# A hybrid attention trunk on one core: two more Strassen-like quads of weight tiles in each layer's down-projection, and their first weight sums made in HBM by DMA

## The chip, the cores and the metric

One NeuronCore of a Trainium2 chip runs the whole program. The metric is the device time of one execution in microseconds, the median of several. Engines are named as in the profile: PE (TensorE), DVE (VectorE), ACT (ScalarE), POOL (GpSimd), SP (SyncE, which here only issues DMAs).

## The reference

Two layers over x of 256 x 2048 in fp32. Each layer adds three sub-layers to x, each between RMSNorms: a mixer of 16 attention heads of three kinds behind one input projection, a cross-attention over 256 memory tokens, and a gated MLP. What the change touches is the last product of the MLP, of 256 x 4096 with a weight of 4096 x 2048:

```
def conv_ffn(h, w_up, conv_w, conv_b, w_down):
    ...
    gate, val = jnp.split(c, 2, axis=-1)
    return (jax.nn.gelu(gate, approximate=True) * val) @ w_down
```

## The kernel before

All weights are laid out on the host as one stream of **pieces** of 128 x 1024 fp32 (512 KB), 344 a layer, in the order of their use. SP loads piece p into the ring `raw` of 8 slots as soon as piece p-8 is free. For exact fp32 products every piece is split in two: ACT copies it into `w_hi` (a rounded form), DVE subtracts that from it into `w_lo`. Both have four slots (`SPL`), and PE multiplies hi x hi, hi x lo and lo x hi. A split waits on ACT until PE has used the split four before it (`split_free`), on DVE for ACT (`hi_ready`), and on PE for DVE (`lo_ready`). Each engine has its own queue in program order; semaphores are all that ties them together.

A layer has these stages: input projection with attention interleaved, output projection, memory keys, queries and values, its output projection, the up-projection (16 groups of 8 pieces) and the down-projection (64 pieces). In the up stage POOL makes one step of the convolution for each group (`up_c`, from DVE's `up_u`).

**The down stage.** It runs in two passes q of 1024 output columns, each of two groups of 512. Weight rows come in blocks j = 0 to 15 of 256, so a pass has 16 pairs of pieces (j, left) and (j, right). An ordinary pair costs PE 2 x 12 matmuls of 128 x 512. For the j in `SEVEN` the pair is instead handled as a **quad**: its two pieces are a 2 x 2 block matrix, and seven products instead of eight, as in Strassen's scheme, do the work, 21 matmuls in place of 24. This needs sums of the activations (made in the up stage, kept in HBM, loaded into `comb` by SP) and sums of the weights. A quad takes four splits, called A (the left piece), D (half of the right one), B (the first two weight sums) and C (two further sums). The weight sums are made by DVE in `psum_b` (an SBUF tile in spite of its name): `first_sums` adds two 128 x 512 pairs in one instruction, `other_sums` makes the other two one after the other. `PASS_HEAD`, `PASS_MID` and `PASS_TAIL` give the order of the blocks; from them come `DOWN_SPLITS` (88 splits of the stage) and `SEVEN_AT` (where the quads start). Between two quads there is always an ordinary pair. At the end of each pass DVE merges the product sums into the accumulators (`merge_sums`, `merge_odd`, `merge_even`), using `psum_b` too. Behind split 20 of the stage, ACT also issues the load of the last gain (`gain_f`, 1 MB) and loads a new activation table.

Of the kernel before, what the change touches and what calls it, by code (L numbers as in the profile page):

```python
# [414 lines left out]
def build(nc, stream, x_in, x_t_in, mem_in, mem_t_in, pos_in, consts_in, cols_in, rows_in, lam_in, gains_in, out):  # L415
    with ExitStack() as ctx:
# [74 lines left out]
        psum_b = sb("psum_b", [P, 4, 512], 88 * K)  # L491
# [170 lines left out]
        b_sums = sem("b_sums")  # L662
        m1_copied = sem("m1_copied")
# [94 lines left out]
        bias_hbm0 = nc.dram_tensor("bias_hbm0", (4 * H_A, 4, 8 * P), F32, kind="Internal").ap()  # L758
        comb_hbm = nc.dram_tensor("comb_hbm", (DEPTH * COMBS, P, 4 * 2 * P), F32, kind="Internal").ap()
# [8 lines left out]
        def _(sp):  # L768
# [24 lines left out]
            for l in range(DEPTH):  # L793
                for r in range(1 if l == 0 else l * rounds, l * rounds + narrow_rounds):
                    for j in range(4 if r == 1 else 0, RAW):
                        p = (r - l * rounds) * RAW + j
                        w = piece_width(p)
                        sp.wait_ge(lo_ready, raw_done(l, p - RAW))
                        sp.dma_start(raw[:, j, 0:w], stream[r * RAW + j][:, 0:w]).then_inc(landed[j], 16)
                with sp.Fori(l * rounds + narrow_rounds, l * rounds + P_DOWN // RAW + 1) as r:  # L800
                    for j in range(RAW):
                        sp.wait_ge(lo_ready, r * RAW + (l * (NSPLITS - NPIECES) + j + 1 - RAW))
                        sp.dma_start(raw[:, j, :], stream[r * RAW + j]).then_inc(landed[j], 16)

                def load_comb(n):

                    _, _, j, _, _ = DOWN_SPLITS[SEVEN_AT[n] - P_DOWN]
                    sp.wait_ge(*pieces_used(l, P_DOWN if n < 2 else SEVEN_AT[n - 2] + 4))
                    sp.wait_ge(comb_put, 16 * (l * COMBS + j // 2 + 2))
                    sp.dma_start(comb[:, n % 2].rearrange("p a b s -> p (a b s)").bitcast(F32),  # L810
                                 comb_hbm[l * COMBS + j // 2]).then_inc(comb_got[n % 2], 16)

                for p in range(P_DOWN + RAW, NPIECES):
                    sp.wait_ge(lo_ready, raw_done(l, p - RAW))
                    sp.dma_start(raw[:, p % RAW, :], stream[l * NPIECES + p]).then_inc(landed[p % RAW], 16)
                    for n, s in enumerate(SEVEN_AT):
                        if p == max(P_DOWN + RAW, P_DOWN + DOWN_SPLITS[s - P_DOWN][4] + 2):
                            load_comb(n)
# [530 lines left out]
        def _(act):  # L1349
# [48 lines left out]
            for l in range(DEPTH):  # L1398
# [4 lines left out]
                def split_down(s):  # L1403
# [8 lines left out]
                    elif kind == "D":  # L1412
                        act.wait_ge(*raw_landed(l, P_DOWN + i))
                        act.wait_ge(split_free, l * NSPLITS + s + 1)
                        act.activation(w_hi[:, s % SPL, 0:512], raw[:, i % RAW, 512:1024], ACT.Copy).then_inc(hi_ready, 1)
                    else:
                        n = l * len(SEVEN_AT) + seven(s - 2 if kind == "B" else s - 3)
                        act.wait_ge(b_sums, 3 * n + (1 if kind == "B" else 3))
                        act.wait_ge(split_free, l * NSPLITS + s + 1)
                        c = 0 if kind == "B" else 2  # L1420
                        act.activation(w_hi[:, s % SPL, :], psum_b[:, c:c + 2, :].rearrange("p a n -> p (a n)"),  # L1421
                                       ACT.Copy).then_inc(hi_ready, 1)
# [323 lines left out]

                for s in range(P_DOWN + SPL, NSPLITS + (2 if l < DEPTH - 1 else 0)):
# [24 lines left out]
        def _(dve):  # L1772
# [132 lines left out]
            for l in range(DEPTH):  # L1905
# [3 lines left out]
                def split_down(s):  # L1909
# [11 lines left out]
                    else:  # L1921
                        c = 0 if kind == "B" else 2
                        dve.wait_ge(hi_ready, l * NSPLITS + s + 1)
                        dve.tensor_tensor(w_lo[:, s % SPL, :], psum_b[:, c:c + 2, :].rearrange("p a n -> p (a n)"),
                                          w_hi[:, s % SPL, :].bitcast(F32), ALU.subtract).then_inc(lo_ready, 1)

                def first_sums(s):

                    ra, rb = [(P_DOWN + DOWN_SPLITS[s - P_DOWN + d][4]) for d in range(2)]
                    assert ra % RAW + 1 == rb % RAW  # L1930
                    n = seven(s)
                    if n == 0:
# [8 lines left out]
                def other_sums(s):

                    ra, rb = [(P_DOWN + DOWN_SPLITS[s - P_DOWN + d][4]) % RAW for d in range(2)]
                    n = 3 * (l * len(SEVEN_AT) + seven(s))
                    dve.wait_ge(b_sums, n + 1)
                    dve.tensor_tensor(psum_b[:, 2, :], psum_b[:, 0, :], raw[:, rb, 512:1024], ALU.add).then_inc(b_sums, 1)
                    dve.wait_ge(b_sums, n + 2)
                    dve.tensor_tensor(psum_b[:, 3, :], psum_b[:, 2, :], raw[:, ra, 512:1024], ALU.add).then_inc(b_sums, 1)
# [11 lines left out]
                def merge_odd(q):  # L1960
# [4 lines left out]
                    dve.tensor_tensor(acc(l, g, 0), acc(l, g, 0), psum_b[:, 0, :], ALU.add)  # L1965
                    st.done(dve.tensor_tensor(acc(l, g, 1), acc(l, g, 1), psum_b[:, 2, :], ALU.add))
                    dve.sem_inc(odd_merged, 1)

                def merge_even(q):
# [4 lines left out]
                    st.done(dve.tensor_tensor(acc(l, g, 1), acc(l, g, 1), psum_b[:, 1, :], ALU.subtract))  # L1974
# [432 lines left out]
                for s in range(P_DOWN + SPL, NSPLITS + (1 if l < DEPTH - 1 else 0)):  # L2407
# [28 lines left out]
        def _(pool):  # L2436
# [37 lines left out]
            for l in range(DEPTH):  # L2474
# [20 lines left out]

                pool.wait_ge(*item_done(l, ("O", HEADS - 1)))
# [14 lines left out]
                with pool.Fori(0, UPG // 2) as i:  # L2511
                    for half in range(2):
# [11 lines left out]
                        ins.then_inc(up_aff_ready, 1)  # L2524

# [128 lines left out]
```

## Time and profile before

| | |
|---|---|
| median of 3 runs | 1966.92 us (1966.91 to 1967.28) |
| profiled execution: its own time | 1967.23 us |
| span of the profile, first to last instruction | 1965.4 us |
| PE busy | 1952.6 us (99%) |
| DVE, ACT, POOL busy | 1506.6, 1138.2, 187.2 us |
| HBM traffic | 200 GB/s over the span |

The span lacks about 2 us around the first and last instruction. Busy time on PE is that of matmuls which overlap each other; the time from the start of one to the start of the next is what a run of them costs. The first layer's down stage runs from about 815 to 985 us, the second one's from about 1791 us to the end.

### The profile page before, as it was taken

What the parts mean: (1) busy time and instruction counts of PE and PEld (TensorE: products, weight loads), DVE (VectorE), ACT (ScalarE), POOL (GpSimd) and SP (SyncE); (2) the same over time, 40 slices, a digit from 0 to 9 for tenths busy, and PEclk for the clock granted to TensorE, in tenths of its full rate; (3) what the DMA queues carried; (4) which work ended last, traced back from release to release, by engine and by line L of the source; (5) the groups of instructions that cost most, each with busy time, mean ns of one, the idle gap of its engine ahead of it and who ended that gap; (6) DMA issues with size and microseconds to landing.
All of it is one profiled execution on the core that took longest, in us unless ns stands there. A gap on an engine that the chain in (4) does not pass through costs nothing.

```text
span 1965.4 us, 30737 instructions
## 1 busy us (share of the span) xinstructions
PE 1952.6 (99%) x10655; PEld 1680.0 (85%) x10655; DVE 1506.6 (77%) x2326; ACT 1138.2 (58%) x1770; POOL 187.2 (10%) x212
## 2 busy tenths in 40 slices
PE   9999999999999999999999999999999999999998
PEld 8888888888888888888888888888888888888886
DVE  7857777857777777788876577768587777778888
ACT  7655566657555555555566655556565555554654
POOL 0010000001222222200000000000012222222000
PEclk9999999999999999999999999999999999999999
DMA  8674558544656666576656444665446666565773
GB/s 319 200 204 155 170 211 241 198 152 169 202 192 207 198 206 200 203 274 240 220 150 229 153 155 160 213 218 196 155 153 205 203 201 209 188 205 210 267 251 135
DMA packets 111490, 393.94 MB, mean 200 GB/s; under 512 B 13140, under 2 KB 14560, under 8 KB 110048
## 3 DMA queue, kind: packets, MB, share of 16 engines
q1 hardware_dynamic: 105632, 368.36, 56.3%
q10 hardware_dynamic: 4448, 20.58, 2.7%
q0 software_dynamic: 1312, 3.70, 0.8%
q8 instruction: 61, 1.00, 0.2%
q14 instruction: 37, 0.30, 0.0%
HBM read 382.35 MB, written 10.24 MB: 200 GB/s over the span
## 4 chain that ended last, share of the span: by engine, by line
PE 98%; DVE 1%; issue 0%; ACT 0%; DMA 0%; DVEq 0%; SPq 0%; ACTq 0%
PE ps L971 24%; PE ps L974 12%; PE ps L881 12%; PE ps L883 11%; PE ps L882 11%; PE ps L893 11%; PE ps L896 5%; PE ps L1298 2%; PE ps L1297 2%; PE ps L1299 2%; PE ps L845 1%; PE ps L1248 1%; PE ps L1236 0%; PE ps L1234 0%; PE ps L1272 0%; PE ps L1260 0%
## 5 line engine op out<-in xcount | busy, mean ns | idle before, releaser
L1778 DVE TENSOR_TENSOR w_lo<-raw,w_hi 128x1024 fp32r<-128x1024 f32 (+2 forms) x660 | 778.6, 1187 | 323.0 <-ACT w_hi L1354 316.9
L1354 ACT ACTIVATE w_hi<-raw 128x1024 fp32r<-128x1024 f32 (+2 forms) x660 | 672.0, 1028 | 345.2 <-PE ps L974 219.7
L971 PE MATMUL ps<-h_t,w_hi 128*128 128x512 f32 x2032 | 639.0, 396 | 0.1
L974 PEld LDWEIGHTS ps<-h_t,w_lo 128*128 128x128 f32 x2032 | 382.1, 188 | 89.7
L974 PE MATMUL ps<-h_t,w_lo 128*128 128x256 f32 x2032 | 399.2, 278 | 0.0
L971 PEld LDWEIGHTS ps<-h_t,w_hi 128*128 128x128 f32 x2032 | 309.3, 189 | 0.3 <-DVE h_t L1796 0.3
L893 PE MATMUL ps<-h_t,w_hi 128*128 128x512 f32 x768 | 246.8, 403 | 0.0
L896 PEld LDWEIGHTS ps<-h_t,w_lo 128*128 128x128 f32 x768 | 144.3, 188 | 33.8
L2522 POOL TENSOR_SCALAR up_c<-up_u,cw 128x256 f32<-128x256 f32 x128 | 130.1, 1027 | 369.6 <-DVE up_u L2356 369.6
L896 PE MATMUL ps<-h_t,w_lo 128*128 128x256 f32 x768 | 151.2, 278 | 0.0
L883 PE MATMUL ps<-w_hi,act_t 128*128 128x512 f32 x320 | 124.5, 389 | 0.0
L881 PE MATMUL ps<-w_hi,act_t 128*128 128x512 f32 x320 | 124.5, 389 | 0.0
L882 PE MATMUL ps<-w_lo,act_t 128*128 128x512 f32 x320 | 124.5, 389 | 0.0
L893 PEld LDWEIGHTS ps<-h_t,w_hi 128*128 128x128 f32 x768 | 118.6, 189 | 1.7 <-DVE w_lo L1778 0.7
L881 PE MATMUL ps<-w_hi,h_t 128*128 128x512 f32 (+2 forms) x310 | 110.5, 356 | 0.1
L883 PE MATMUL ps<-w_hi,h_t 128*128 128x512 f32 (+2 forms) x310 | 108.2, 349 | 0.0
L882 PE MATMUL ps<-w_lo,h_t 128*128 128x512 f32 (+2 forms) x310 | 108.0, 348 | 0.0
L881 PE MATMUL ps<-w_hi,o_t 128*128 128x512 f32 x256 | 101.1, 395 | 0.0
L883 PE MATMUL ps<-w_hi,o_t 128*128 128x512 f32 x256 | 99.8, 390 | 0.0
L882 PE MATMUL ps<-w_lo,o_t 128*128 128x512 f32 x256 | 99.7, 390 | 0.0
L1421 ACT ACTIVATE w_hi<-psum_b 128x1024 fp32r<-128x1024 f32 x48 | 50.9, 1061 | 80.3 <-PE ps L883 80.0
L1699 ACT ACTIVATE s_sb<-s_sb,nmax 128x128 f32<-128x128 f32 x80 | 35.8, 449 | 76.2 <-DVE nmax L2295 75.4
(372 smaller groups left out, 2838.4 us busy)
## 6 DMA issues: line engine op xcount, KB each, us to landing
raw<-stream SPq DMA_DIRECT2D x640, 512.0 KB, 4.3
comb<-comb_hbm SPq DMA_DIRECT2D x24, 512.0 KB, 4.8
comb_hbm<-comb_out ACTq DMA_DIRECT2D x14, 512.0 KB, 6.1
raw<-stream SPq DMA_DIRECT2D x24, 288.0 KB, 3.4
raw<-stream SPq DMA_DIRECT2D x16, 262.0 KB, 6.0
gain_a<-gains_in ACTq DMA_DIRECT2D x4, 1024.0 KB, 6.5
m_x<-mem_t_in ACTq DMA_DIRECT2D x2, 2048.0 KB, 11.6
x<-x_in SPq DMA_DIRECT2D x4, 512.0 KB, 13.4
```

The lines of the kernel that those rows point to most:

```text
L881: pe.matmul(dst, s_hi, hi[:, j, :], start=f, stop=False, skip_group_check=True)
L882: pe.matmul(dst, s_hi, lo[:, j, :], start=False, stop=False, skip_group_check=True)
L883: mm = pe.matmul(dst, s_lo, hi[:, j, :], start=False, stop=e, skip_group_check=True)
L893: pe.matmul(acc(l, g, nt), hi[:, j, nt * P:(nt + 1) * P], src[:, c, :, :], start=f, stop=False, skip_group_check=True)
L896: mm = pe.matmul(acc(l, g, nt)[:, SEQ:2 * SEQ], lo[:, j, nt * P:(nt + 1) * P], src[:, c, 0, :], start=False, stop=e, skip_group_check=True)
L971: pe.matmul(ps[:, 4 * half + nt, :], hi[:, cc, nt * P:(nt + 1) * P], h_t[:, c, :, :], start=(c == 0), stop=False, skip_group_check=True)
L974: mm = pe.matmul(ps[:, 4 * half + nt, SEQ:2 * SEQ], lo[:, cc, nt * P:(nt + 1) * P], h_t[:, c, 0, :], start=False, stop=(c == KC - 1), skip ...
L1297: pe.matmul(dst, s_hi, hi, start=first, stop=False, skip_group_check=True)
L1354: act.activation(w_hi[:, slot, 0:width], raw[:, rslot, 0:width], ACT.Copy).then_inc(hi_ready, 1)
L1421: act.activation(w_hi[:, s % SPL, :], psum_b[:, c:c + 2, :].rearrange("p a n -> p (a n)"), ACT.Copy).then_inc(hi_ready, 1)
L1778: dve.tensor_tensor(w_lo[:, slot, 0:width], raw[:, rslot, 0:width], w_hi[:, slot, 0:width].bitcast(F32), ALU.subtract).then_inc(lo_ready, 1)
L2522: ins = pool.tensor_scalar(up_c[:, nt, :], up_u[:, nt, :], cw[:, 4 * nt + 2:4 * nt + 3], cw[:, 4 * nt + 3:4 * nt + 4], ALU.mult, ALU.add)
```

## The change

1. `SEVEN` gets a seventh block, j = 12: 14 quads a layer for 12. The order of the blocks changes, and in each pass there are now two places where two quads follow one another without an ordinary pair between. The stage has 92 splits.
2. The first weight sums are no longer made by DVE. POOL issues, for each quad, a copy of two half pieces from the stream into `b_hbm` and then, when that has landed, an accumulating DMA that adds the other halves. Eight quads are made at steps spread over the attention, output and memory stages (`SUMS_EARLY`), six in the up stage, one DMA a group; POOL's loop over the up groups is written out.
3. ACT issues a DMA (`load_sums`) that brings the sums of a quad, 512 KB, into `psum_b`, which is now two buffers, used in turn. `other_sums` stays on DVE and waits for that load; for a row of two quads both quads' other sums are made ahead of the first.
4. For the D piece of a quad only the half that is still used is loaded.

```diff
-SEVEN = [0, 2, 4, 6, 8, 10]
-PASS_HEAD, PASS_TAIL = [1, 3], [[14, 15], [12, 14, 15]]
-PASS_MID = [[5, 0, 7, 2, 9, 4, 11, 6, 13, 8, 12, 10], [0, 5, 2, 7, 4, 9, 6, 11, 8, 13, 10]]
+SEVEN = [0, 2, 4, 6, 8, 10, 12]
+PASS_HEAD, PASS_TAIL = [1, 3], [[14, 15], [13, 14, 15]]
+PASS_MID = [[5, 0, 7, 2, 4, 9, 6, 8, 11, 10, 13, 12], [0, 5, 2, 4, 7, 6, 8, 9, 10, 11, 12]]
+SUMS_EARLY = [(n, 48 + 11 * n) for n in range(4)] + [(4 + n, P_OUT + 6 + 11 * n) for n in range(3)] + [(7, P_MEMV)]
...
-        psum_b = sb("psum_b", [P, 4, 512], 88 * K)
+        psum_b = [sb(f"psum_b{i}", [P, 4, 512], at) for i, at in enumerate((88 * K, 104 * K))]
...
-                    sp.dma_start(raw[:, p % RAW, :], stream[l * NPIECES + p]).then_inc(landed[p % RAW], 16)
+                    c = 512 if P_DOWN + DOWN_FREED[p - P_DOWN] - 1 in SEVEN_AT else 0
+                    sp.dma_start(raw[:, p % RAW, c:], stream[l * NPIECES + p][:, c:]).then_inc(landed[p % RAW], 16)
...
+                def load_sums(n):
+
+                    m = l * len(SEVEN_AT) + n
+                    if n < 2:
+                        act.wait_ge(*pieces_used(l, P_DOWN - 4 * (1 - n)))
+                        act.wait_ge(b_made, 16 * (l + 1) * len(SEVEN_AT))
+                    else:
+                        act.wait_ge(lo_ready, l * NSPLITS + SEVEN_AT[n - 2] + 4)
+                    if DOWN_SPLITS[SEVEN_AT[n] - P_DOWN][1] == 1 and n % 2 == 0:
+                        act.wait_ge(odd_merged, 2 * l + 1)
+                        act.wait_ge(even_merged, 2 * l + 1)
+                    act.dma_start(psum_b[n % 2][:, 0:2, :], b_hbm[m]).then_inc(b_got[n % 2], 16)
+
+                load_sums(0)
                 for s in range(P_DOWN + SPL, NSPLITS + (2 if l < DEPTH - 1 else 0)):
                     up_tail(UPG // 2 - 1, 1, tail_at(s))
                     split_down(s)
+                    if s == P_DOWN + SPL:
+                        load_sums(1)
+                    for n in range(2, len(SEVEN_AT)):
+                        merged = DOWN_SPLITS[SEVEN_AT[n] - P_DOWN][1] == 1 and n % 2 == 0
+                        if s == max(SEVEN_AT[n - 2] + 5, down_end(1) + SPL + 1 if merged else 0):
+                            load_sums(n)
                     if s == P_DOWN + 20:
...
-                def first_sums(s):
+                def other_sums(s):
 
                     ra, rb = [(P_DOWN + DOWN_SPLITS[s - P_DOWN + d][4]) for d in range(2)]
-                    assert ra % RAW + 1 == rb % RAW
                     n = seven(s)
-                    if n == 0:
-                        dve.wait_ge(*pieces_used(l, P_DOWN - 4))
-                    else:
-                        dve.wait_ge(lo_ready, l * NSPLITS + SEVEN_AT[n - 1] + 4)
+                    m = 2 * (l * len(SEVEN_AT) + n)
+                    sums = psum_b[n % 2]
+                    if n > 1:
+                        dve.wait_ge(lo_ready, l * NSPLITS + SEVEN_AT[n - 2] + 4)
+                    dve.wait_ge(*first_sums(l, n))
+                    dve.wait_ge(*raw_landed(l, rb))
+                    dve.tensor_tensor(sums[:, 2, :], sums[:, 0, :], raw[:, rb % RAW, 512:1024], ALU.add).then_inc(b_sums, 1)
+                    dve.wait_ge(b_sums, m + 1)
                     dve.wait_ge(*raw_landed(l, ra))
...
-                    if s + 2 in SEVEN_AT:
-                        first_sums(s + 2)
-                    if s + 1 in SEVEN_AT:
+                    if s + 1 in SEVEN_AT and s - 3 not in SEVEN_AT:
                         other_sums(s + 1)
+                        if s + 5 in SEVEN_AT:
+                            other_sums(s + 5)
...
+                def sums_copy(n):
+
+                    m = l * len(SEVEN_AT) + n
+                    p = l * NPIECES + P_DOWN + DOWN_SPLITS[SEVEN_AT[n] - P_DOWN][4]
+                    pool.dma_start(b_hbm[m].rearrange("p a n -> a p n"), stream[p:p + 2, :, 0:512]).then_inc(b_put, 16)
+
+                def sums_add(n):
...
+                    pool.wait_ge(b_put, 16 * (m + 1))
+                    pool.dma_start(b_hbm[m].rearrange("p a n -> a p n"), stream[p + 1].rearrange("p (a n) -> a p n", n=512),
+                                   accum_op=ALU.add).then_inc(b_made, 16)
...
-                with pool.Fori(0, UPG // 2) as i:
+                for i in range(UPG // 2):
...
+                        n = len(SUMS_EARLY) + i
+                        if n < len(SEVEN_AT):
+                            (sums_add if half else sums_copy)(n)
```

**ACT, first layer's down stage, from the split of an ordinary pair to two quads later.** In the rows, an ACTIVATE from raw is the hi split of a piece (128x512: of a D piece), one from psum_b the B and C splits. Before, around the gain load:

```order
L1354 ACTIVATE w_hi<-raw 128x1024 x3
L1415 ACTIVATE w_hi<-raw 128x512
L1421 ACTIVATE w_hi<-psum_b 128x1024
L1753 DMA gain_f<-gains_in 128x2048
L1754 ACT_TABLE_LOAD
L1754 ACTIVATE lamv<-ident 128x1
L1421 ACTIVATE w_hi<-psum_b 128x1024
L1354 ACTIVATE w_hi<-raw 128x1024 x3
```

Of the change, the same place; psum_b_99 and psum_b_100 are the two buffers, and the three rows from the gain load on stand between the two splits 20 and 21 of an ordinary pair:

```order
L1365 ACTIVATE w_hi<-raw 128x1024
L1787 DMA gain_f<-gains_in 128x2048
L1788 ACT_TABLE_LOAD
L1788 ACTIVATE lamv<-ident 128x1
L1365 ACTIVATE w_hi<-raw 128x1024
L1772 DMA psum_b_99<-b_hbm 128x1024
L1365 ACTIVATE w_hi<-raw 128x1024
L1426 ACTIVATE w_hi<-raw 128x512
L1435 ACTIVATE w_hi<-psum_b_100 128x1024 x2
L1365 ACTIVATE w_hi<-raw 128x1024
L1426 ACTIVATE w_hi<-raw 128x512
L1772 DMA psum_b_100<-b_hbm 128x1024
```

The load of the second quad's sums (L1772, into psum_b_99) now stands behind split 21, four rows after the gain load.

**DVE, the same place.** A TENSOR_TENSOR into w_lo is a split's subtraction, one into psum_b makes weight sums. Before:

```order
L1778 TENSOR_TENSOR w_lo<-raw,w_hi 128x1024
L1938 TENSOR_TENSOR psum_b<-raw 128x1024
L1778 TENSOR_TENSOR w_lo<-raw,w_hi 128x1024
L1946 TENSOR_TENSOR psum_b<-psum_b,raw 128x512
L1948 TENSOR_TENSOR psum_b<-psum_b,raw 128x512
L1778 TENSOR_TENSOR w_lo<-raw,w_hi 128x1024
L1919 TENSOR_TENSOR w_lo<-raw,w_hi 128x512
L1924 TENSOR_TENSOR w_lo<-psum_b,w_hi 128x1024 x2
```

Of the change, splits 20 and 21, the sums of two quads, and the four splits of the first of them:

```order
L1812 TENSOR_TENSOR w_lo<-raw,w_hi 128x1024 x2
L1972 TENSOR_TENSOR psum_b_100<-psum_b_100,raw 128x512
L1975 TENSOR_TENSOR psum_b_100<-psum_b_100,raw 128x512
L1972 TENSOR_TENSOR psum_b_99<-psum_b_99,raw 128x512
L1975 TENSOR_TENSOR psum_b_99<-psum_b_99,raw 128x512
L1812 TENSOR_TENSOR w_lo<-raw,w_hi 128x1024
L1953 TENSOR_TENSOR w_lo<-raw,w_hi 128x512
L1959 TENSOR_TENSOR w_lo<-psum_b_100,w_hi 128x1024 x2
```

The first sums (L1938) are gone, and the sums of the second quad (psum_b_99) are made before the first quad's splits.

## Rows read from the trace of the kernel before

**Rows 1.** The page's first part: busy us, share of the span, instructions.
```profile
PE 1952.6 (99%) x10655; PEld 1680.0 (85%) x10655; DVE 1506.6 (77%) x2326; ACT 1138.2 (58%) x1770; POOL 187.2 (10%) x212
```

**Rows 2.** Waits of PE's weight loads: us in total, times, longest.
```profile
PEld ps L845 <- DVE x L2075: 2.0, 2, 1.0
...
PEld ps L881 <- DVE w_lo L1778: 1.1, 3, 0.4
...
PEld ps L893 <- DVE w_lo L1778: 0.7, 2, 0.3
```

**Rows 3.** Timeline of PE, first quad: start, us, instruction.
```profile
831.62 0.39 PE L1297 MATMUL ps<-w_hi,act_t 128*128 128x512 f32 x1
831.84 0.39 PE L1298 MATMUL ps<-w_lo,act_t 128*128 128x512 f32 x1
...
832.98 0.39 PE L1297 MATMUL ps<-w_hi,comb 128*128 128x512 f32 x1
```

**Rows 4.** Timeline of DVE around a quad.
```profile
857.01 1.22 DVE L1778 TENSOR_TENSOR w_lo<-raw,w_hi 128x1024 fp32r<-128x1024 f32 x1
858.14 0.69 DVE L1946 TENSOR_TENSOR psum_b<-psum_b,raw 128x512 f32<-128x512 f32 x1
858.86 0.69 DVE L1948 TENSOR_TENSOR psum_b<-psum_b,raw 128x512 f32<-128x512 f32 x1
859.47 1.22 DVE L1778 TENSOR_TENSOR w_lo<-raw,w_hi 128x1024 fp32r<-128x1024 f32 x1
860.61 0.68 DVE L1919 TENSOR_TENSOR w_lo<-raw,w_hi 128x512 fp32r<-128x512 f32 x1
861.21 1.22 DVE L1924 TENSOR_TENSOR w_lo<-psum_b,w_hi 128x1024 fp32r<-128x1024 f32 x1
```

**Rows 5.** Stretches of the down stage; last three: granted clock, DMA share, GB/s.
```profile
817.00:826.00 9.00, 9.00 (x42) 7.44 (x41) 8.36 (x8) 3.70 (x4) 5.55 (x4) 1.00 0.97 370
847.00:856.00 9.00, 9.00 (x41) 7.45 (x40) 8.07 (x10) 6.41 (x8) 0.00 (x0) 1.00 0.91 355
826.00:885.00 59.00, 59.00 (x262) 48.88 (x261) 52.81 (x59) 34.85 (x38) 0.39 (x1) 1.00 0.69 253
```

**Rows 6.** Timeline of ACT and its queue behind split 20.
```profile
849.55 1.06 ACT L1421 ACTIVATE w_hi<-psum_b 128x1024 fp32r<-128x1024 f32 x1 [2.09 <-PE ps L883]
849.63 0.36 ACTq L1753 DMA_DIRECT2D gain_f<-gains_in  x1
850.63 1.28 ACT L1754 ACT_TABLE_LOAD   x1
851.93 0.20 ACT L1754 ACTIVATE lamv<-ident 128x1 f32<-128x1 f32 x1
852.27 1.06 ACT L1421 ACTIVATE w_hi<-psum_b 128x1024 fp32r<-128x1024 f32 x1
```

**Rows 7.** Landing of the comb loads, then of gain_f in each layer.
```profile
DMA to landing us min/median/max: 3.6/4.8/7.1
...
DMA to landing us min/median/max: 7.8/7.8/7.8
...
DMA to landing us min/median/max: 8.6/8.6/8.6
```

**Rows 8.** POOL: its DMA issues (ns), and its timeline in the up stage.
```profile
L2492 POOL DMA_DIRECT2D f_k<-f_hbm x2: 548/558/567, 131.6 to 1058.6; - x2
...
511.08 3.94 POOL L2522 TENSOR_SCALAR up_c<-up_u,cw 128x256 f32<-128x256 f32 x4 [10.27 <-DVE up_u L2356]
522.09 1.01 POOL L2516 COPY cw<-cols 128x16 f32 x1 [7.07 <-DVE up_a L2371]
```

**Rows 9.** The page's DMA queues: packets, MB, share of 16 engines.
```profile
q1 hardware_dynamic: 105632, 368.36, 56.3%
```

**Rows 10.** DMA issues: KB each, median us to landing.
```profile
raw<-stream SPq DMA_DIRECT2D x640, 512.0 KB, 4.3
...
m_x<-mem_t_in ACTq DMA_DIRECT2D x2, 2048.0 KB, 11.6
```

**Rows 11.** PE's last matmul, and the stretches behind it.
```profile
1956.81 0.39 PE L883 MATMUL ps<-w_hi,act_t 128*128 128x512 f32 x1
...
1957.00:1959.00 2.00, 0.20 (x1) 0.00 (x0) 1.96 (x6) 0.98 (x3) 0.00 (x0) 1.00 0.84 326
1959.00:1961.00 2.00, 0.00 (x0) 0.00 (x0) 1.89 (x6) 0.00 (x0) 0.00 (x0) 0.75 0.54 199
```

More of the change, by code:

```diff
@@ L662, in build @@
         b_sums = sem("b_sums")
+        b_put = sem("b_put")
+        b_made = sem("b_made")
+        b_got = [sem(f"b_got{i}") for i in range(2)]
         m1_copied = sem("m1_copied")
@@ L1417, in split_down @@
                         n = l * len(SEVEN_AT) + seven(s - 2 if kind == "B" else s - 3)
-                        act.wait_ge(b_sums, 3 * n + (1 if kind == "B" else 3))
+                        if kind == "B":
+                            act.wait_ge(*first_sums(l, n - l * len(SEVEN_AT)))
+                        else:
+                            act.wait_ge(b_sums, 2 * n + 2)
                         act.wait_ge(split_free, l * NSPLITS + s + 1)
                         c = 0 if kind == "B" else 2
-                        act.activation(w_hi[:, s % SPL, :], psum_b[:, c:c + 2, :].rearrange("p a n -> p (a n)"),
+                        act.activation(w_hi[:, s % SPL, :], psum_b[n % 2][:, c:c + 2, :].rearrange("p a n -> p (a n)"),
                                        ACT.Copy).then_inc(hi_ready, 1)
@@ L1922, in split_down @@
                         c = 0 if kind == "B" else 2
+                        n = seven(s - 2 if kind == "B" else s - 3)
                         dve.wait_ge(hi_ready, l * NSPLITS + s + 1)
-                        dve.tensor_tensor(w_lo[:, s % SPL, :], psum_b[:, c:c + 2, :].rearrange("p a n -> p (a n)"),
+                        dve.tensor_tensor(w_lo[:, s % SPL, :], psum_b[n % 2][:, c:c + 2, :].rearrange("p a n -> p (a n)"),
                                           w_hi[:, s % SPL, :].bitcast(F32), ALU.subtract).then_inc(lo_ready, 1)
-                def first_sums(s):
+                def other_sums(s):
@@ L1941, in other_sums @@
[L1941 to L1948, printed above, removed]
+                    m = 2 * (l * len(SEVEN_AT) + n)
@@ new lines, in other_sums @@
+                    sums = psum_b[n % 2]
[5 more added lines that the diff above has]
+                    dve.wait_ge(b_sums, m + 1)
+                    dve.wait_ge(*raw_landed(l, ra))
+                    dve.tensor_tensor(sums[:, 3, :], sums[:, 2, :], raw[:, ra % RAW, 512:1024], ALU.add).then_inc(b_sums, 1)
@@ L1950, in merge_sums @@
                 def merge_sums(q):
-                    w5, w7, x57 = [psum_b[:, c, :] for c in range(3)]
+                    w5, w7, x57 = [psum_b[0][:, c, :] for c in range(3)]
                     dve.wait_ge(*pieces_used(l, LAST_SEVEN[q] + 1))
@@ L1964, in merge_odd @@
                         dve.wait_ge(*pieces_used(l, GROUP_END[g]))
-                    dve.tensor_tensor(acc(l, g, 0), acc(l, g, 0), psum_b[:, 0, :], ALU.add)
-                    st.done(dve.tensor_tensor(acc(l, g, 1), acc(l, g, 1), psum_b[:, 2, :], ALU.add))
+                    dve.tensor_tensor(acc(l, g, 0), acc(l, g, 0), psum_b[0][:, 0, :], ALU.add)
+                    st.done(dve.tensor_tensor(acc(l, g, 1), acc(l, g, 1), psum_b[0][:, 2, :], ALU.add))
                     dve.sem_inc(odd_merged, 1)
@@ L1973, in merge_even @@
                     dve.tensor_tensor(acc(l, g, 0), acc(l, g, 0), m1_s[:], ALU.add)
-                    st.done(dve.tensor_tensor(acc(l, g, 1), acc(l, g, 1), psum_b[:, 1, :], ALU.subtract))
+                    st.done(dve.tensor_tensor(acc(l, g, 1), acc(l, g, 1), psum_b[0][:, 1, :], ALU.subtract))
                     dve.sem_inc(even_merged, 1)
@@ L2501, in _ @@
                     pool.dma_start(rm_t[:], r_hbm[1].partition_broadcast(P)).then_inc(rm_got, 16)
+                for n, p in SUMS_EARLY:
+                    if p >= P_OUT:
+                        pool.wait_ge(*pieces_used(l, p))
+                        sums_copy(n)
+                        sums_add(n)
                 for tb in range(TB):
```

15 lines of the change are left out of this document (12 added, 3 removed).

## The prediction

> **What bounds the kernel now.** I read the page first: PE is busy 1952.6 of 1965.4 us, every other engine at most 77% [rows 1]. Then PE's waits: a handful of short ones, and of those for a weight tile that DVE had not finished splitting only some 2 us in the whole program [rows 2]. PE alone sets the time, because its feeders run ahead by the four slots of `w_hi`/`w_lo`. So the change can win only by what it takes off PE, and it loses whatever makes a split later than PE wants it. I count the down stage in splits s, 0 for its first; split s may start on ACT when PE has finished split s-4.
>
> **What it takes off PE.** A quad has 7 products of 3 matmuls where two ordinary pieces have 24: 3 matmuls less. In a run of matmuls the starts lie 0.227 us apart (831.62 to 832.98 for six) [rows 3]; the "mean ns" of 390 is the latency of one and would be the wrong price. An ordinary piece is 12 x 0.227 = 2.72 us of PE, a quad 21 x 0.227 = 4.76, its four splits A, D, B, C being 1.36, 0.68, 1.36, 1.36. There are 14 quads a layer for 12, so 4 x 3 x 0.227 = **2.7 us less** in all, 0.14%. That is under the 0.2% (3.9 us) which a measurement of this kernel can tell from no change.
>
> **What it takes off DVE.** The first sums (L1938) go: 24 x 1.22 us. Each quad keeps two half sums, 0.72 us apart, then 0.6 to the next, and four subtractions, 1.13 us apart for a whole tile (0.6 for a half) [rows 4]. DVE works 52.8 of 59 us in the down stage [rows 5], but PE waits for it almost never, so this relief buys nothing by itself. Work per quad falls from 6.5 to 5.3 us; two quads in a row are 10.7 us of DVE against 9.5 of PE, which the four slots and an ordinary pair (2.3 of DVE, 5.4 of PE) on either side absorb.
>
> **What it adds: a load that must arrive.** The 512 KB of first sums now come by a DMA that ACT issues (load_sums) and DVE waits for in other_sums. Where a quad stands alone, or first of two, four splits or more (8 us of PE) lie between the two. For the second of two the order shows otherwise: load_sums of the second quad stands right behind the ACT split s-5, and DVE forms the sums of both quads right behind its own split s-5, ahead of the first quad's four. So DVE stands still until the load has landed, and PE uses up its slots: what can come late is split 12, 22, 56 and 66. This is so for the second quads at s = 16, 26, 60 and 70, each layer. I worked the four out by the durations above.
>
> *s = 16.* PE starts split 6 at 831.62 [rows 3], so it ends split 7 at 833.7 and wants split 12 at 831.62 + 4.76 + 5.44 = 841.8. Hi 10 and 11 run on ACT at 833.3 and 834.3; a DMA behind an activation is issued 0.08 us after that activation starts (849.55, 849.63) [rows 6], so at 834.4. From landing to PE's start of split 12 it takes 0.72 + 0.65 (sums) + 1.22 (split) + 0.3 = 2.9 us. The load is in time if it lands in 4.5 us. The nearest rows are the loads of `comb`, the same 512 KB in 4 KB rows: 3.6 to 7.1, median 4.8 [rows 7]. But SP holds its next load (comb of this quad) until PE has finished split 9, so this one travels alone and I take the low end: no wait. s = 60 (PE's split 56) is the same with 4.7 us. At s = 70 (split 66) comb and two raw loads left within 2 us before it, so about 4.9 us, 0.3 us late. Together I take **0.3 us a layer**; with 5.5 us everywhere they would give 2.6, with 3.6 nothing.
>
> *s = 26.* PE wants split 22 at 831.62 + 4.76 + 5.44 + 9.52 + 5.44 = 856.8. Here ACT is late: behind hi 20 stand the gain_f load, the table load and a small activation, and the next hi comes 2.72 us after (849.55 to 852.27) [rows 6]. Hi 20 waits for split 16 of PE, done at 848.1, so hi 21 starts at 850.9 and the load is issued at 850.95. It would have to land by 856.8 - 2.9 = 853.9, in 2.9 us; no 512 KB load of comb was under 3.6. At 3.6 PE stands 0.7 us, at 4.8 1.9 us. And it isn't alone: gain_f, 1 MB, left 2.75 us earlier on the same ACT queue and took 7.8 and 8.6 us in the two layers [rows 7]; comb, half a raw tile and two whole ones left SP's queue in the 3 us before. Counting gain_f from 848.2 it lands at 856.0 to 856.8; 512 KB at the 355 to 370 GB/s that the stage reaches when full [rows 5] are 1.45 us more, so the sums land near 857.5 to 858.3, 6.5 to 7.3 us after issue; the extra traffic of this stage pushes to the upper end and beyond. Then PE starts split 22 at 861.2 and not at 856.8: I take **4.5 us a layer**, bounds 0.7 and 5.7 (a landing of 8.6 us, gain_f's longest).
>
> By the Trainium skill, "DMA: Bandwidth & Descriptors", Queues, rings and completion order, each engine keeps one ring for a queue row and consumes its descriptors in order. By that the sums can't overtake gain_f; without it, the estimate would be the 1.9 us. No row of before has two loads close together on ACT's queue.
>
> **The rest.** The copies and adds in HBM are POOL's: 28 of each. A DMA issue costs POOL about 0.55 us [rows 8], and in the up stage it stands idle 7 and 10 us in each group [rows 8]; early in the layer it is idle for tens of us. All are done before the down stage needs them (the last add is in the twelfth group of 16). Their bytes go through engines 56% busy with SP's loads [rows 9], and raw loads leave eight pieces ahead (about 20 us) and need 4.3 [rows 10]: hidden, zero; bound below nothing, above some 3 us in all, were one of them to hold the x blocks that POOL adds at 451 us. The unrolled POOL loop, the extra ACT issues (0.36 us beside a running activation) and the half raw loads (256 KB less a quad) change nothing that PE waits for.
>
> **The sum.** -2.7 + 2 x 4.5 + 2 x 0.3 = +6.9 on the profiled run's own 1967.2, which is 0.3 over the median: 1973.8.
>
> **The clock.** After PE's last matmul (end 1957.2) the granted clock went from its 2.4 GHz level to the 1.2 GHz one: it is 1.00 until 1959 and 0.75 over 1959 to 1961, so it fell at about 1960, 2.8 us after [rows 11]. A stand of 4.5 us is longer. If it falls and takes as long to come back, 2.8 us run at half speed, 1.4 us lost each time. I give it one chance in three for each layer and add 0.7: **1974.5**.
> The Trainium skill, "TensorE: Matmul & The Clock Gate", The HAM clock gate, says that the clock drops to 1.2 GHz after an idle stretch and returns after a busy one; this trace's end agrees with the first half.
>
> **Rivals.**
> - *Not slower: the load lands in time.* It decides at the split 22 alone: if the two queues share so that the sums come within 4.8 us of issue, the stand is 1.9 us or less a layer, the others nil: -2.7 + 3.8 = +1, down to -2.7 + 1.4 = -1.3. 1965.5 to 1970.8. For it: half the comb loads land in 4.8. Against: gain_f's own 8 us just ahead. 0.17.
> - *All second quads late.* If loads take 5.5 to 6.5 us everywhere (comb took up to 7.1), s = 16, 60 and 70 give 1.0 to 2.0 each: 2 x 3 x 1.5 = 9 more, 1982. Against: SP is silent at two of the three. 0.1.
> - *HBM work in the way.* The copies and adds have an outermost dimension of 2; should only two engines carry each, it would be slow. One of the 16 engines takes 0.563 x 16 x 1965.4 / 105632 = 0.17 us for a packet of 3.5 KB [rows 9], so 256 KB on each of two are 12.5 us, and an add perhaps twice that. Raw loads share those two engines, and POOL waits for each copy. With 20 us of lead it holds; where it doesn't (mem_t_in, 11.6 us [rows 10], loads under the copies of the out stage) PE would stand 3 us or more: 1977 to 1982. 0.08. The Trainium skill, "DMA: Bandwidth & Descriptors", Why a DMA increments its semaphore by 16 and not by 1, says just this, that a DMA is cut over at most as many engines as divide its outermost dimension; no run here shows it yet.
> - *Faster by over 0.2%* needs 3.9 us, more than the 2.7 that there is plus the waits of PE that DVE's relief could end. 0.02.
> - The forecast, a long stand at split 22 and little elsewhere, clock or not: 0.63, own range 1971 to 1979.
>
> **Numbers.** Slower than 1970.8: 0.63 + 0.1 + 0.08 = 0.81; same 0.17; faster 0.02. The range has to reach into the first rival and into the others: 1968 to 1981.
>
> **What would show it.** Right: in the changed profile PE has one gap of 4 to 5 us a layer, where split 22 of the down stage begins (near 857 and 1836 us), behind an ordinary pair, with DVE waiting for the DMA psum_b<-b_hbm just before; that load 6.5 us or longer, the others 3.6 to 5; PE's matmuls 12 fewer; busy DVE down by some 16 us; a down stage some 3 us longer a layer. Wrong: no such gap (then the queue order was not what I took), PE waits in the out, memory or up stages, or gaps at splits 12, 56, 66 as large as that at 22.

## The result

The changed kernel takes 2002.1 us (median of 4, 1999.9 to 2003.2) against 1967.0: 1.77% slower, ratio 1.0177 [1.0164, 1.0189]. The direction was forecast; the size, 35 us for 7.5, was not, and the time lies 21 us above the range. The profiled execution has a span of 2001.4 us, 36.0 more than that of before.

The page of the changed kernel, part 1 and then part 3 (queues: packets, MB, share of 16 engines), with the line of packet sizes:

```profile
PE 1959.1 (98%) x10643; PEld 1682.9 (84%) x10643; DVE 1494.5 (75%) x2318; ACT 1145.1 (57%) x1778; POOL 270.2 (13%) x268
...
DMA packets 203012, 433.88 MB, mean 217 GB/s; under 512 B 89812, under 2 KB 91232, under 8 KB 201568
...
q0 software_dynamic: 88224, 33.67, 8.8%
```

PE has its 12 matmuls less (10655 in [rows 1]), and DVE works 12 us less (some 16 were forecast). What is new stands in PE's waits (us in total, times, longest), for [rows 2]:

```profile
PE ps L856 <- POOL x L2560: 19.3, 1, 19.3
PE ps L1308 <- DVE w_lo L1812: 10.9, 4, 5.2
```

The second line is the stand of the forecast; the first is one of 19.3 us which it did not have. The first starts of PE's instructions on two lines place them (L982 is the up stage's matmul, L971 before; L1308 a quad's, L1297 before). Before:

```profile
L971 PE MATMUL ps<-h_t,w_hi x2032: 390/396/499, 459.1 to 1790.6; 128*128 128x512 f32 x185
...
L1297 PE MATMUL ps<-w_hi,act_t x72: 388/389/390, 831.6 to 1940.0; 128*128 128x512 f32 x72
```

and in the changed kernel:

```profile
L982 PE MATMUL ps<-h_t,w_hi x2032: 390/396/774, 478.7 to 1819.2; 128*128 128x512 f32 x185
...
L1308 PE MATMUL ps<-w_hi,act_t x84: 389/389/796, 853.1 to 1976.1; 128*128 128x512 f32 x84
```

The first layer's up stage starts 19.6 us late; the first quad 21.5 us late; the second layer's up stage ends 28.6 us late (1819.2 to 1790.6), the program 36.0. So the turn to the first up stage costs 21.5 us with what follows it, and each down stage some 7 (28.6 - 21.5 and 36.0 - 28.6). The second layer's turn costs nothing.

**The turn.** POOL's timeline there (start, us, instruction, idle before and what ended it):

```profile
408.20 1.91 POOL L2534 DMA_DIRECT2D b_hbm<-stream  x1 [40.00 <-DMA b_hbm<-stream]
409.29 1.90 POOL L2527 DMA_DIRECT2D b_hbm<-stream  x1
445.52 1.90 POOL L2534 DMA_DIRECT2D b_hbm<-stream  x1 [34.33 <-DMA b_hbm<-stream]
446.62 1.88 POOL L2527 DMA_DIRECT2D b_hbm<-stream  x1
473.88 1.89 POOL L2534 DMA_DIRECT2D b_hbm<-stream  x1 [25.37 <-DMA b_hbm<-stream]
475.00 3.55 POOL L2560 TENSOR_TENSOR x<-y_a,x 128x256 f32<-128x256 f32 x4
```

L2527 is a copy, L2534 the add behind it. In the kernel before, POOL comes to the two blocks of x that it adds (L2560, there L2507) at 451 us:

```profile
451.13 1.49 POOL L2507 TENSOR_TENSOR x<-y_a,x 128x256 f32<-128x256 f32 x2 [116.95 <-ACT y_a L1594]
```

Now it waits 25 to 40 us for each copy and falls behind its schedule: the eighth quad's copy is issued at 446.6 us (in x1_wide, below, where POOL keeps up, at 399.2). It comes to x at 475 us. PE needs these blocks for the transposes of the next stage. In the stretch before that, the granted clock and the DMA share (the last columns: granted clock, DMA share, GB/s):

```profile
462.00:478.00 16.00, 0.08 (x1) 0.08 (x2) 0.00 (x1) 0.00 (x0) 4.12 (x6) 0.51 0.15 25
478.00:482.00 4.00, 4.00 (x14) 3.51 (x15) 4.00 (x5) 1.78 (x3) 1.68 (x2) 0.50 0.49 106
```

In the first of them all work but POOL's and its DMAs' stands still; the DMAs keep 0.15 of the 16 engines busy, the time of a little over two, and move 25 GB/s. The clock has gone to its 1.2 GHz level and stays there while PE works again until 482.8 us. A stretch of 4 us inside the stand, 466 to 470, has nothing but this queue, one add and one copy still under way:

```profile
DMA packets 51, 0.10 MB, mean 26 GB/s; under 512 B 0, under 2 KB 0, under 8 KB 51
...
q0 software_dynamic: 51, 0.10, 14.2%
```

14.2% of 16 engines are 2.3, with no small packet among the 51. The add (issued at 445.52) and the copy (446.62) both landed some 27 us after their issue, so both were under way here.

**The down stages.** ACT's queue and DVE around split 22 of the first layer, for [rows 6]; then the landing of the load issued at 870.67:

```profile
869.76 0.34 ACTq L1787 DMA_DIRECT2D gain_f<-gains_in  x1
870.67 0.33 ACTq L1772 DMA_DIRECT2D psum_b<-b_hbm  x1
870.76 1.28 ACT L1788 ACT_TABLE_LOAD   x1
...
DMA to landing us min/median/max: 10.3/10.3/10.3
```

```profile
875.10 0.69 DVE L1975 TENSOR_TENSOR psum_b<-psum_b,raw 128x512 f32<-128x512 f32 x1
881.02 0.69 DVE L1972 TENSOR_TENSOR psum_b<-psum_b,raw 128x512 f32<-128x512 f32 x1 [5.23 <-DMA psum_b<-b_hbm]
```

The sums land at 880.97, 0.05 us before DVE takes them; PE stands from 878.0 to 883.6. The clock falls here too, in the stretches behind it:

```profile
880.00:883.00 3.00, 0.00 (x0) 0.00 (x0) 1.95 (x3) 0.00 (x0) 0.00 (x0) 0.86 0.75 301
883.00:889.00 6.00, 5.37 (x13) 4.21 (x14) 4.71 (x6) 1.69 (x2) 0.00 (x0) 0.50 0.32 96
889.00:892.00 3.00, 3.00 (x15) 2.48 (x14) 1.57 (x2) 1.80 (x2) 0.00 (x0) 1.00 0.54 165
```

PE starts again at 883.63 us, and its next 12 steps from one matmul to the next take 5.28 us, where 12 x 0.227 are 2.72: 2.6 us lost behind a stand of 5.6. In the second layer 13 steps behind the stand of 5.2 take 5.71 us for 2.95, 2.8 lost.

### The profile page after: what moved, and what is told of

It reads as the page before. It is cut to its first block, busy times and chain, and to the rows that moved or that the text cites. A ratio compares the mean times of both kernels' runs of the same rounds, so it can differ in the third digit from the quotient of the medians.

```text
span 2001.4 us, 30741 instructions
## 1 busy us (share of the span) xinstructions
PE 1959.1 (98%) x10643; PEld 1682.9 (84%) x10643; DVE 1494.5 (75%) x2318; ACT 1145.1 (57%) x1778; POOL 270.2 (13%) x268
## 3 DMA queue, kind: packets, MB, share of 16 engines
q0 software_dynamic: 88224, 33.67, 8.8%
## 4 chain that ended last, share of the span: by engine, by line
PE 72%; DMA 9%; DVE 2%; ACT 0%; POOL 0%; issue 0%; DVEq 0%; ACTq 0%; POOLq 0%
PE ps L982 24%; PE ps L985 12%; PE ps L892 7%; PE ps L894 7%; PE ps L893 7%; DMA b_hbm<-stream 6%; PE ps L904 5%; PE ps L907 3%; PE ps L1308 2%; PE ps L1309 2%; PE ps L1310 2%; DMA psum_b<-b_hbm 2%; DMA r_hbm<-rst_m 1%; PE ps L856 1%; DVE w_lo L1812 0%
## 5 line engine op out<-in xcount | busy, mean ns | idle before, releaser
L982 PE MATMUL ps<-h_t,w_hi 128*128 128x512 f32 x2032 | 640.2, 396 | 0.0
L982 PEld LDWEIGHTS ps<-h_t,w_hi 128*128 128x128 f32 x2032 | 310.2, 189 | 0.0
L2534 POOL DMA_DIRECT2D b_hbm<-stream x28 | 53.6, 1915 | 532.8 <-DMA b_hbm<-stream 532.8
L892 PE MATMUL ps<-w_hi,act_t 128*128 128x512 f32 x288 | 112.1, 389 | 0.0
L893 PE MATMUL ps<-w_lo,act_t 128*128 128x512 f32 x288 | 112.0, 389 | 0.0
L894 PE MATMUL ps<-w_hi,act_t 128*128 128x512 f32 x288 | 112.0, 389 | 0.0
L1435 ACT ACTIVATE w_hi<-psum_b 128x1024 fp32r<-128x1024 f32 x56 | 59.4, 1061 | 76.4 <-PE ps L894 68.2
## 6 DMA issues: line engine op xcount, KB each, us to landing
b_hbm<-stream POOLq DMA_DIRECT2D x56, 512.0 KB, 35.6
```

The lines of the kernel that those rows point to most:

```text
L892: pe.matmul(dst, s_hi, hi[:, j, :], start=f, stop=False, skip_group_check=True)
L893: pe.matmul(dst, s_hi, lo[:, j, :], start=False, stop=False, skip_group_check=True)
L894: mm = pe.matmul(dst, s_lo, hi[:, j, :], start=False, stop=e, skip_group_check=True)
L982: pe.matmul(ps[:, 4 * half + nt, :], hi[:, cc, nt * P:(nt + 1) * P], h_t[:, c, :, :], start=(c == 0), stop=False, skip_group_check=True)
L1435: act.activation(w_hi[:, s % SPL, :], psum_b[n % 2][:, c:c + 2, :].rearrange("p a n -> p (a n)"), ACT.Copy).then_inc(hi_ready, 1)
L2534: pool.dma_start(b_hbm[m].rearrange("p a n -> a p n"), stream[p + 1].rearrange("p (a n) -> a p n", n=512), accum_op=ALU.add).then_inc(b_ma ...
```

## The experiments

All are edits of the changed kernel, timed against the kernel before (1967.0 to 1967.1 us on the same chip).

**x1_wide: the copies and adds cut over more engines.** The edit of the add also names a longest row of 4096 (`max_dma_last_dim`).

```diff
-pool.dma_start(b_hbm[m].rearrange("p a n -> a p n"), stream[p:p + 2, :, 0:512])
+pool.dma_start(b_hbm[m], stream[p:p + 2, :, 0:512].rearrange("a p n -> p a n"))
...
-pool.dma_start(b_hbm[m].rearrange("p a n -> a p n"), stream[p + 1].rearrange("p (a n) -> a p n", n=512),
+pool.dma_start(b_hbm[m], stream[p + 1].rearrange("p (a n) -> p a n", n=512), max_dma_last_dim=4096,
```

> The copies and adds in HBM are written with the 128 partitions outermost on both sides, so that they can be cut over 16 DMA engines; nothing else changes. Theory 'two engines': the landing of these DMAs, median 28 us over all of them in the changed kernel, falls under 10 us, POOL no longer waits for long, the stand of PE of 19.6 us at 458 us goes with the slow clock behind it, and the time falls by 21 us from 2002 to about 1981. Rival 'HBM to HBM and adding are slow by nature, or starved by the weight stream': landing stays at 20 us or more, the stand stays and the time stays near 2002. The stands of 5.6 and 5.2 us at split 22 of the two down stages stay under both.

1980.3 us, ratio 1.0068 [1.0051, 1.0085]: 21.8 us less. Its DMA issues (KB each, median us to landing) and the queue's line:

```profile
q0 software_dynamic: 9376, 33.06, 7.4%
...
b_hbm<-stream POOLq DMA_DIRECT2D x56, 512.0 KB, 6.9
```

The median is 6.9 us where the changed kernel has 35.6 (my 28 was the median of all DMAs of that tile, the later loads included). The stand in the turn is gone; raw loads are back at a median of 4.4 us from 7.2. The two stands in the down stages are there as before. The bytes are nearly the same; the packets of the queue fall from 88224 to 9376, since the narrow form had also made some 75,000 packets under 512 B. So the form of the DMAs was the cause. The edit changes both the number of engines and these small packets. The stretch 466 to 470 us above has none of the small packets and still moves 26 GB/s at 2.3 engines, so the few engines are enough to make these DMAs slow; how much the small packets added elsewhere was not taken apart.

**x11_adds_wide: only the adds changed so.**

> The changed kernel with only the adds written with the partitions outermost; the copies stay as they are, with 2 outermost. Theory 'copies of 512 KB on two engines take 16 to 20 us by themselves and were stretched to 25 to 44 by the adds still running': copies land in 15 to 22 us, adds under 10, POOL reaches its x blocks in time and the 19.6 us stand goes: about 1981. Rival 'the copies alone are slow enough': the stand stays at several us, 1985 to 2002.

1978.7 us in one execution. The copies landed in 15.7 to 29.1 us (median 18.7), the adds in 6.0 to 9.8. The turn has no stand. From 165 to 176 us a narrow copy is alone on POOL's queue, which takes 8.9% of the 16 engines' time, 1.4 of them; during a copy of x1_wide (162 to 165 us) it takes 66.1%, 10.6 of them. A narrow copy takes over 15 us by itself; with narrow adds it was 17.3 to 45.4, since each add (27.1 to 56.2) still ran under the next copy.

**x2_late7: the eighth quad's copy and add moved out of POOL's way.**

```diff
-SUMS_EARLY = [(n, 48 + 11 * n) for n in range(4)] + [(4 + n, P_OUT + 6 + 11 * n) for n in range(3)] + [(7, P_MEMV)]
+SUMS_EARLY = [(n, 48 + 11 * n) for n in range(4)] + [(4 + n, P_OUT + 6 + 11 * n) for n in range(3)]
```

> The entry (7, P_MEMV) of SUMS_EARLY is taken out, so that the copy and add of the eighth quad are made in the up stage, seven there in place of six. The DMAs stay as slow as they are. Theory 'POOL waits for the copy in front of its x blocks': the 19.6 us stand and its slow clock (together 21.5 us) go, 2002 becomes about 1980.5. Rival 'the traffic itself slows what the turn needs (m_x, gains, raw)': a stand of several us stays before the up stage, time 1985 to 2000.

2007.7 us, ratio 1.0207 [1.0190, 1.0224]: slower than the change, a miss. The turn did lose its stand (POOL adds its x blocks at 453.5 us), with 2.2 us left of PE waiting for x. But seven quads in the up stage put the last add two groups later (of 22 us each), the adds still take 34 to 58 us, and ACT waits for all 14 in front of the down stage, here ahead of up_u:

```profile
833.03 1.02 ACT L1734 ACTIVATE up_u<-ps 128x1024 f32<-128x1024 f32 x1 [14.10 <-DMA b_hbm<-stream]
```

PE waits 17.6 us for it, once in each layer (9.1 the longer), with the clock at its low level behind both. The mechanism of the turn holds; that nothing else waits for these DMAs was false as soon as they moved.

**x3_gain_later: the gain load out of the way of the sums.**

```diff
-                    if s == P_DOWN + 20:
+                    if s == P_DOWN + 32:
```

> The gain_f load and the table load behind it move from split 20 to split 32 of the down stage, behind the load of the seventh quad's sums. Theory 'the sums queue behind gain_f': the psum_b load at split 21 lands in about 5 us and not 10.3, and the stand at split 22 falls from 5.6 and 5.2 us to under 1 us, the clock stays at its high level in both down stages; 5 + 2.2 us a layer less, 2002 becomes about 1988. Rival 'the row of two quads is itself too tight': the stand stays at 2 to 3 us a layer, since the load was to land in 2.9 us; then about 1993.

1989.9 us, ratio 1.0116 [1.0099, 1.0133]: 12.2 less. The clock stays at 1.00 in both down stages. PE's waits at the quads:

```profile
PE ps L1308 <- DVE w_lo L1812: 4.7, 4, 2.4
```

10.9 us became 4.7, at splits 22 and 66. So the queue behind gain_f made most of it, and what is left is the rival's: loads of 6.3 us at split 22 and 7.5 at 66, where some 4.7 were allowed at each (at split 22 not 2.9, since the load is issued 1.8 us earlier than I had it). Both theories have a share. Not all of the 12.2 us is the edit's: the stand in the turn is 17.2 us in this profile and 19.6 in that of the changed kernel. In the down stages the weight loads' waits fall from 12.6 to 6.4 us, and the slow clock (4.7 us by the sums in the section on the prediction) goes.

**x5_gain_dma_only: only the DMA moved, the table load left.**

```diff
+                        act.activation(lamv[:, 5:6], ident[:, 0:1], ACT.Sqrt)
+                    if s == P_DOWN + 32:
                         act.dma_start(gain_f[:], gains_in[l * 3 + 2].partition_broadcast(P)).then_inc(gain_here, 16)
-                        act.activation(lamv[:, 5:6], ident[:, 0:1], ACT.Sqrt)
```

> Only the gain_f DMA moves to split 32; the table load stays behind split 20. Theory 'only the place behind gain_f on ACT's queue costs': as in x3_gain_later, the stand at split 22 is 1 to 2 us in both layers, time 1987 to 1990. Rival 'the table load delays the issue of the sums load by 1.8 us, as the prediction had it': the stand stays 1.8 us longer than in x3_gain_later, 3 to 3.5 us a layer, time about 1992.

1988.2 us (2 executions), ratio 1.0108 [1.0089, 1.0126]. The waits at the quads are 1.0 us at most, 1.5 by the weight loads (L1813 is the splits' line here):

```profile
PE ps L1308 <- DVE w_lo L1813: 2.4, 4, 1.0
```

The table load costs nothing that shows there: the timeline above shows the sums load issued 0.91 us after gain_f, ahead of the table load's start and not behind it.

**x4_apart: each quad's sums right ahead of its own splits.**

```diff
-                    if s + 1 in SEVEN_AT and s - 3 not in SEVEN_AT:
+                    if s + 1 in SEVEN_AT:
                         other_sums(s + 1)
-                        if s + 5 in SEVEN_AT:
-                            other_sums(s + 5)
```

> DVE makes the other sums of each quad right ahead of that quad's own splits, in a row of two as well; gain_f stays at split 20. Theory 'DVE stands in front of the first quad's four splits for the second quad's load': with a load of 10 us issued at the same place DVE does those four splits (4.2 us) first and the stand at split 22 goes, or moves to split 26 with under 1 us; the stands of 0.7 and 1.1 us at split 66 go too: 2002 becomes about 1986. Rival 'DVE has no time left in a row of two': the stand only moves to split 26 or later with 3 us or more; 1995 or above.

1989.7 us, ratio 1.0115 [1.0098, 1.0132], against 1986 expected. The stand at split 22 is gone though gain_f is where it was: DVE splits the first quad while the load is under way. New ones take its place: 0.6 to 0.9 us at splits 26, 60 and 70 and 1.2 us at split 16 in each layer, 6.3 us in all, where DVE comes late by its own work. At split 16 (start, us):

```profile
864.21 0.69 DVE L1972 TENSOR_TENSOR psum_b<-psum_b,raw 128x512 f32<-128x512 f32 x1
864.93 0.69 DVE L1975 TENSOR_TENSOR psum_b<-psum_b,raw 128x512 f32<-128x512 f32 x1
865.54 0.69 DVE L2401 TENSOR_TENSOR act_t<-up_a,act_t 128x512 fp32r<-128x512 f32 x1
866.14 1.22 DVE L1812 TENSOR_TENSOR w_lo<-raw,w_hi 128x1024 fp32r<-128x1024 f32 x1
```

**x6_wide_gain: x1 and x3 together.**

> Both larger mends together: copies and adds with the partitions outermost, gain_f and its table load at split 32. Theory: the stand in the turn and the slow clock are gone everywhere; what is left is the 2.7 us gained against 0 to 3 us a layer at splits 22 and 66, where DVE still waits for a load before the first quad's splits: 1965 to 1970. Rival 'another cost of the HBM work is left over all stages': above 1972.

1967.6 us, ratio 1.0005 [0.9996, 1.0014]: level with the kernel before. The costs of the two causes add up: 21.8 and 12.2 us less alone, 34.5 together. Stands of 1.3 and 0.9 us at split 22 and 0.5 and 1.0 at 66 have eaten the matmuls.

**x8_all: x1, x3 and x4 together.**

> The two mends and DVE's sums of each quad right ahead of its own splits. The stands at splits 12, 22, 56, 66 are gone; the 1.2 us at split 16 of each layer seen in x4_apart stays, where DVE also has the act_t subtraction: 1967.1 - 2.7 + 2.4 = 1966.8. Rival 'the slack is so thin that a stand of 1 us or more turns up elsewhere': 1968 or above.

1969.0 us, ratio 1.0010 [1.0001, 1.0019]; 1966.8 was expected. The 1.2 us at split 16 are there, and so are 0.6 us at splits 26, 60 and 70 of each layer, which the forecast left out though x4_apart had them. Now that the loads come in time, this order of DVE's work costs 1.4 us more than that of x6_wide_gain.

**x9_tail21: and the act_t subtraction later.**

```diff
-            return {P_DOWN + 4: 0, P_DOWN + 6: 2, P_DOWN + 10: 3, P_DOWN + 11: 4, P_DOWN + 12: 5, P_DOWN + 16: 6}.get(s, 1)
+            return {P_DOWN + 4: 0, P_DOWN + 6: 2, P_DOWN + 10: 3, P_DOWN + 11: 4, P_DOWN + 12: 5, P_DOWN + 21: 6}.get(s, 1)
```

> As x8_all, and the act_t subtraction of the last up group (step 6 of up_tail) moves from split 16 to split 21 on ACT and DVE. The 1.2 us at split 16 goes in both layers: 1967.1 - 2.7 = 1964.4, the full worth of the 12 matmuls and the fastest version. Rival 'the matmuls saved are paid back by waits of the merges or the turn': no less than 1966.

1967.9 us, ratio 1.0003 [0.9994, 1.0012]: a miss by 3.5 us. The waits of PE's weight loads:

```profile
PEld ps L1308 <- DVE w_lo L1812: 4.8, 8, 0.6
```

Eight waits of 0.6 us, one at the second quad of each row: the last split of the first quad, 1.4 us of sums and the second quad's first split are more than PE leaves there, while DVE stood idle for 1.49 us two splits earlier.

**x10_between: the second quad's sums in that idle time.**

```diff
                     if s + 1 in SEVEN_AT and s - 3 not in SEVEN_AT:
                         other_sums(s + 1)
-                        if s + 5 in SEVEN_AT:
-                            other_sums(s + 5)
+                    if s + 2 in SEVEN_AT and s - 2 in SEVEN_AT:
+                        other_sums(s + 2)
```

> As x9_tail21, but in a row of two DVE makes the second quad's other sums behind the first quad's B split, where it stood idle for 1.5 us, and not ahead of the second quad's A split, where they cost PE 0.55 us at each of eight places (4.4 us). Theory 'the room is in the row, not at its seam': these eight waits go and the full 2.7 us show: 1967.1 - 2.7 = 1964.4. Rival 'a row of two is short of DVE time wherever the sums stand': waits of the same size move, time stays at 1966.5 to 1968.

**1964.1 us** (1963.8 to 1964.3, 11 runs), ratio 0.9985 [0.9976, 0.9994]: 2.9 us under the kernel before and the fastest version. Its timeline of DVE in the first row of two:

```profile
840.45 1.23 DVE L1959 TENSOR_TENSOR w_lo<-psum_b,w_hi 128x1024 fp32r<-128x1024 f32 x1
841.59 0.69 DVE L1972 TENSOR_TENSOR psum_b<-psum_b,raw 128x512 f32<-128x512 f32 x1
842.31 0.69 DVE L1975 TENSOR_TENSOR psum_b<-psum_b,raw 128x512 f32<-128x512 f32 x1
843.17 1.23 DVE L1959 TENSOR_TENSOR w_lo<-psum_b,w_hi 128x1024 fp32r<-128x1024 f32 x1 [0.17 <-ACT w_hi L1435]
```

The sums stand between the B and the C split and DVE still waits for ACT behind them; PE waits for no split of a quad at all; the short waits that are left are those of before.

**x12_between_only: the same, with gain_f and the table load back at split 20.**

> As x10_between, but gain_f and the table load stay at split 20. The sums load behind gain_f landed 10.3 us after its issue; with the new place of the sums DVE needs it some 8 us after. Theory 'queue behind gain_f': a stand of 1 to 2.5 us a layer shortly after split 24, 1966.5 to 1969. Rival 'with the copies wide the load is in time anyway': 1964.4.

1974.2 us, ratio 1.0038 [1.0025, 1.0051]; a miss by 5. The load still lands in 10.9 us at the longest, and PE waits for the sums 4.0 us in one layer and 0.9 in the other; besides it waits 1.5 us in each at an ordinary piece near split 21. This run is not the clean test that it was meant to be. ACT waits for the act_t step ahead of the gain load, and that step now stands behind DVE's split 20:

```profile
851.06 0.34 ACTq L1787 DMA_DIRECT2D gain_f<-gains_in  x1
851.43 1.28 ACT L1788 ACT_TABLE_LOAD   x1 [2.26 <-DVE act_t L2401]
851.58 0.57 ACTq L1772 DMA_DIRECT2D psum_b<-b_hbm  x1
```

So the sums load leaves at 851.58 us, 2.4 later than in x10_between (849.19), and the stand of 4.0 has part of that in it. The profiled execution, 1971.6 us, is the fastest of the five. The other four take 2.5 to 3.5 us more and have a mean granted clock of 0.997 to 0.998 for its 0.999; what happened in them no profile shows.

## Why the prediction was wrong

- **What bounds, and the matmuls.** Right. PE bounds; 12 matmuls at 0.227 us are 2.7 us, and x10_between, which has none of the new waits, gains 2.9 (1.2 to 4.7 at the bounds of its interval).
- **DVE's relief.** Right that it buys nothing. "Two quads in a row, which the four slots and an ordinary pair absorb" was too generous: x9_tail21 shows 0.6 us at each seam, from the place of the sums and not their amount.
- **The stand at split 22.** The place, the mechanism (DVE waits ahead of the first quad's splits for a load queued behind gain_f) and the order of size were right: 5.6 and 5.2 us for the 4.5 forecast. The load is issued 1.8 us earlier than I had it, since ACT issued it ahead of the table load's start, and takes 10.3 us for 6.5 to 7.3. The earlier issue bought nothing, as gain_f was in front either way: counted from gain_f's issue the sums landed after 11.2 and 10.7 us, where the forecast has 9.3 to 10.1. The mis-sized term is the 1.45 us from gain_f's landing to that of the sums, which measured 2.6 and 2.5. Of splits 12, 56 and 66 only 66 cost anything, 0.7 us in one layer and 1.1 in the other, for 0.3.
- **The clock.** It fell in both layers, for which I had one chance in three each, and cost 2.2 and 2.5 us, for 1.4. These are what is left of the two down stages when the rest is taken off; by the steps of the matmuls they are 2.6 and 2.8 (7.1 = 5.6 + 0.7 - 1.4 + 2.2 in the first down stage, 7.4 = 5.2 + 1.1 - 1.4 + 2.5 in the second). Two chances in three of 1.4 us would have been 0.9, not the 0.7 that was added. With this the down stages account for 7.1 + 7.4 = 14.5 us, twice the 7.5 that the forecast gave for everything.
- **The step that failed: "The rest... hidden, zero; above some 3 us in all".** It cost 21.5 us. The rival "HBM work in the way" had the cause, two engines for each DMA, and the victim stood in the same paragraph (the x blocks that POOL adds at 451 us); but it had 8 chances in 100, its price ended at 1982 us, and my eye was on the raw loads, whose lead did hold. The wait that was left out is POOL's own, in program order ahead of its x blocks. A copy was put at 12.5 us and an add at twice that. Measured, a copy takes 17 to 45 us and an add 27 to 56, which runs on under the next copy, so that POOL passes a quad in 27 to 43 us (copies at 339.7, 366.3, 409.3, 446.6 us). In the first layer it starts the last four of the early quads at 339.7 us, behind the row of factors of the memory, which only this layer makes, and is through at 475: 135 us, where x is due after 111. In the second it starts at 1289.3 us, some 54 us earlier in the layer (its x blocks lie 975.5 us apart before, and 28.6 are delay), and reaches x at 1455.3, in time. The prediction's own sign of being wrong, a wait of PE outside the down stage, is what the trace shows. x1_wide, where the step holds as it was meant, takes 1980.3 us, just inside the range.
- **Two small slips in the rivals.** 9 us on 1973.8 are 1982.8, not 1982, and the first rival's own sum ends at 1968; 1970.8 is the bound of "same".

By the Trainium skill, "DMA: Bandwidth & Descriptors", Why a DMA increments its semaphore by 16 and not by 1, an outermost dimension of 2 leaves two engines to a DMA. The traces agree: the time of 1.4 engines for a narrow copy alone on its queue (x11_adds_wide), of 2.3 with a copy and an add under way and nothing else; and x1_wide, which has 128 outermost, landed in 6.9 us for 35.6. I had that rule in hand, and priced the queue that shares the engines but not the engine that waits for the result.

## What to carry to other kernels

A DMA that "only" prepares something early is free until an engine waits for it in order: list what stands behind that wait in its queue, and run its schedule with the landing time of the narrow form, not with the bytes over the full rate. Put the dimension that the engines are cut over outermost (here the 128 partitions): the same bytes landed five times sooner. And where an engine with 10% of slack (DVE works 52.8 of 59 us in the down stage before) must fit in extra work, its place inside the pattern decides: the same two instructions cost 0.6 us at a seam and nothing one split earlier.

## What the runs showed of the hardware

- A copy of 512 KB from HBM to HBM with 2 outermost takes 15.7 us or more, an adding one 27 us or more; with 128 outermost the adding ones took 6.0 to 9.8 us (x11_adds_wide), the copies 4.0 to 10.2 (x1_wide).
- A DMA behind an ACT_TABLE_LOAD in ACT's program was issued before the table load started (870.67, 870.76).
- A 512 KB load issued 0.9 us behind one of 1 MB on the same ACT queue landed after 10.3 and 9.8 us; the median of all 28 is 4.8.
- Behind the stands of 5.6 and 5.2 us PE's granted clock was at its 1.2 GHz level through some 5 us of work; around the stands of 0.7 to 2.9 us in the down stages of x3_gain_later, and around that of 4.0 us in the profile of x12_between_only, it was at 2.4 GHz throughout.
